# A hybrid decoder step on one core: resident output weights, a ring of six expert rows, diagonals made by VectorE

## The reference, cut to what matters

```python
h = rmsnorm(x, norm1_g); p = h @ w_in                    # 1024 -> 3072 columns
mix = concat([conv_mixer(p), rwkv_mixer(p), sb_attention(p)])
x = x + mix @ w_out                                      # w_out: 1024 x 1024
h2 = rmsnorm(x, norm2_g)
x = x + peer(h2, w_query, sub_keys, u_tab, v_tab)
y = rmsnorm(x, final_g)

def peer_block(xb, w_query, sub_keys, u_tab, v_tab):     # 128 tokens, 8 heads
    s = queries of xb against 2 x 128 keys per head
    s1, i1 = top_k(s[:, :, 0], 16); s2, i2 = top_k(s[:, :, 1], 16)
    top_s, pos = top_k(all 256 sums of s1 and s2, 16)
    e = the 16 experts of pos, out of 16384
    gate = softmax(top_s)
    act = gelu(einsum('thkd,td->thk', u_tab[e], xb))
    return einsum('thk,thkd->td', gate * act, v_tab[e])
```

## Time and profile before

| | us |
|---|---|
| median of 3 runs | 3605.5 |
| lowest and highest run | 3588.62 and 3607.0 |
| the profiled execution's own time | 3601.69 |
| its span, first to last instruction | 3599.9 |
| PE / DVE / ACT / POOL busy in the span | 2793.4 / 2582.6 / 1309.0 / 1381.4 |
| bytes moved by DMA | 1253.82 MB |
| mean granted TensorE clock | 0.866 of full speed |

### The profile page before, as it was taken

One profiled execution on the slowest core, in us unless ns is written; L12 is line 12 of the kernel. 1 busy time (PEld: TensorE's weight loads), 2 busy tenths in 40 slices (PEclk: granted clock), 3 DMA queues, 4 the chain that ended last, 5 costly groups with the idle time before them and its releaser, 6 DMA issues.

```text
span 3599.9 us, 52601 instructions
## 1 busy us (share of the span) xinstructions
PE 2793.4 (78%) x19158; PEld 1375.9 (38%) x19158; DVE 2582.6 (72%) x6413; ACT 1309.0 (36%) x2869; POOL 1381.4 (38%) x1199
## 2 busy tenths in 40 slices
PE   8999877777678767786887678787878777767657
PEld 4555464334244324432443244334433333423211
DVE  2477234878777877788778776887788767677775
ACT  2222122435332543254325532563256323233322
POOL 0000001344453446344544463445444645354443
PEclk9999998888789888988898888888888798788888
DMA  3123354999999999999999999999999999899998
GB/s 96 39 62 92 109 180 178 381 403 384 371 413 400 412 399 408 408 402 416 416 404 398 391 411 399 399 409 414 402 404 405 406 416 410 312 410 410 414 408 342
DMA packets 253683, 1253.82 MB, mean 348 GB/s; under 512 B 63144, under 2 KB 90832, under 8 KB 117744
## 3 DMA queue, kind: packets, MB, share of 16 engines
q0 software_dynamic: 160256, 1132.54, 77.8%
q1 hardware_dynamic: 93168, 117.92, 9.6%
HBM read 1226.84 MB, written 23.53 MB: 347 GB/s over the span
## 4 chain that ended last, share of the span: by engine, by line
PE 27%; DMA 26%; DVE 23%; ACT 5%; issue 4%; POOL 1%; SPq 0%; DVEq 0%; ACTq 0%; POOLq 0%
PE peer_y L2471 13%; DMA uv_first<-in_peer_uv,expert 13%; DMA uv_rows<-in_peer_uv,expert 10%; PE peer_s L2037 5%; DVE uv_first L1775 5%; DVE uv_rows L1775 4%; DMA w_out_rows<-in_w_out 2%; PE scan L2151 2%; PE beside L2077 2%; ACT diag L2012 2%; DVE same L1377 1%; DVE same L1379 1%; DVE pick L1381 1%; DVE weights L1401 1%; ACT L2004 1%
## 5 line engine op out<-in xcount | busy, mean ns | idle before, releaser
L1333 POOL DMA_INDIRECT uv_first<-in_peer_uv,expert x604 | 715.8, 1185 | 1039.9 <-PE peer_y L2471 776.6
L2471 PE MATMUL peer_y<-uv_first,diag 64*64 64x512 f32 x4688 | 742.1, 746 | 390.5 <-ACT diag L2012 376.9
L1775 DVE CUSTOM_DVE_ANT_0 uv_first<-uv_first,p_h 128x1024 f32<-128x1024 f32 x604 | 728.6, 1222 | 204.6 <-DMA uv_first<-in_peer_uv,expert 203.0
L2471 PE MATMUL peer_y<-uv_rows,diag 64*64 64x512 f32 x3504 | 563.2, 751 | 295.8 <-ACT diag L2012 289.1
L1333 POOL DMA_INDIRECT uv_rows<-in_peer_uv,expert x452 | 520.3, 1151 | 676.0 <-PE peer_y L2471 596.9
L1775 DVE CUSTOM_DVE_ANT_0 uv_rows<-uv_rows,p_h 128x1024 f32<-128x1024 f32 x452 | 546.1, 1223 | 139.2 <-DMA uv_rows<-in_peer_uv,expert 138.3
L2004 ACT ACTIVATE gelu<-hidden 128x2 f32<-128x2 f32 x528 | 107.3, 203 | 1209.2 <-DVE hidden L1775 1206.9
L2012 ACT ACTIVATE diag<-p_ident,weights 128x128 f32<-128x128 f32 x1024 | 355.1, 394 | 489.5 <-DVE weights L1401 488.8
L2471 PEld LDWEIGHTS peer_y<-uv_first,diag 64*64 64x64 f32 x4688 | 181.6, 158 | 739.0 <-ACT diag L2012 525.1
L2471 PEld LDWEIGHTS peer_y<-uv_rows,diag 64*64 64x64 f32 x3504 | 136.2, 158 | 561.4 <-ACT diag L2012 406.4
L593 PE MATMUL proj<-mix,w_in_tile 128*128 128x512 f32 x672 | 295.4, 598 | 0.0
(11 more groups left out here) (460 smaller groups left out, 3955.8 us busy)
## 6 DMA issues: line engine op xcount, KB each, us to landing
w_out_rows<-in_w_out SPq DMA_DIRECT2D x50, 512.0 KB, 8.2
w_in_tile<-in_w_in SPq DMA_DIRECT2D x24, 512.0 KB, 3.4
uv_first<-in_peer_uv,expert POOLq DMA_INDIRECT x604
uv_first<-in_w_query SPq DMA_DIRECT2D x8, 1024.0 KB, 7.2
uv_rows<-in_peer_uv,expert POOLq DMA_INDIRECT x452
scan_in<-scratch_scan_in SPq DMA_DIRECT2D x15, 480.0 KB, 8.3
pages_ring<-scratch_k_tiles SPq DMA_DIRECT2D x36, 192.0 KB, 14.2
pages_ring<-out_v_new SPq DMA_DIRECT2D x36, 192.0 KB, 18.5
```

The costliest lines, as they stand in the source:

```text
L1333: pool.indirect_dma_start(out=uv(m, ALL, slice(0, 2 * D)), out_offset=None, in_=io["peer_uv"], in_offset=bass.IndirectOffsetOnAxis(ap=expe ...
L1775: nc.vector.tensor_tensor_reduce(out=uv(m, ALL, slice(0, D)), in0=uv(m, ALL, slice(0, D)), in1=h2[:, b % 2, :], scale=1.0, scalar=0.0, op0 ...
L2471: ins = nc.tensor.matmul(Y[r][rows[j], :], diag[rows[r], m % (2 * GP), rows[r]], uv(m, rows[r], slice(D + j * 512, D + (j + 1) * 512)), st ...
```

## The change

It has these parts.
- **w_out**: all eight slabs have a place of their own (`wo`, [128, 8, 1024]) and are loaded once, by two DMAs of 2 MB. `weights`, `w_out_last` and `w_out_half` are gone.
- **The ring**: six slots in place of seven, one tensor (`uv_ring`).
- **Page slots**: six in place of eight, three for key tiles and three for value tiles. The samples' pages go round by `page_slot`, and beats K_PAGES and V_PAGES are lists.
- **Diagonals**: `weigh` makes them on VectorE, two `tensor_scalar` of 128x64 a group with two per-partition factors (gelu and gate), six slots; ScalarE makes none, and `weights` is gone.
- **Scores**: `choose` reads them in PSUM; `keep` is gone. `score(t + 3)` moves from q = 1 to q = 4 and waits for the last reading of the turn before.
- **final_g**: no longer spread by the load; TensorE spreads it over the rows (`final_gain`, 8 small products) into two PSUM banks once a block, and `normalise` reads it there, at turn 2, q = 6.
- **The samples' state** and other tiles of the samples' attention lie in one tensor with the attention's (`att_units`). The state is loaded before block 6 goes on, and `scan_sample` takes a step every second beat from beat 9.
- In SP's stream the second `scan_load` of a block comes before the store of y.

```diff
-    RING = 7
-    GP = 2
-    PAGES = 8
+    GP, DIAGS = 2, 6
+    PAGES = 6
...
-    K_PAGES, V_PAGES = -4, 5
-    CLOSE, X, SPREAD, H2, TURN, H2T = 24, 33, 34, 35, 35, 37
+    K_PAGES, V_PAGES = (-4, -3, -2, -1, 0, 1, 5, 6), (7, 8, 9, 10, 11, 12, 17, 18)
+    CLOSE, X, SPREAD, H2, TURN, H2T = 24, 33, 34, 35, 35, 38
...
-    S_SCAN, S_TURN = 35, DB - 2
+    W_OUT = DC
+    S_SCAN, S_TURN = 9, DB - 2
...
-    scored = lambda t, q: t + 3 if q == 1 else TURNS
-    kept = lambda t, q: t + 3 if q == 7 else TURNS
+    scored = lambda t, q: t + 3 if q == 4 else TURNS
...
-            if b == S_TURN and n - S_SCAN in range(S_STEPS):
-                scan_sample(n - S_SCAN)
+            if b == S_TURN and n - S_SCAN in range(0, 2 * S_STEPS, 2):
+                scan_sample((n - S_SCAN) // 2)
...
+            for n in range(2):
+                half = slice(n * DC // 2, (n + 1) * DC // 2)
+                sp.dma_start(wo[:, half, :], io["w_out"][:, half, :]).then_inc(wo_in[n], 16)
...
-                if g >= 2:
-                    dve.wait_ge(diag_done, GP * (g - 1))
-                nc.vector.tensor_tensor(wgt[:, g % 2, :], gel[:, g % 2, :], gate[:, t % 4, q * GP:(q + 1) * GP], ALU.mult)\
-                    .then_inc(weights_done, 1)
+                eye, n = (ident4, NS) if last(b) else (ident2, HT)
+                for k in range(GP):
+                    m = g * GP + k
+                    if m >= DIAGS:
+                        dve.wait_ge(uv_free, m - DIAGS + 1)
+                    nc.vector.tensor_scalar(diag[:, m % DIAGS, 0:n], eye[:, 0:n], gel[:, g % 2, k:k + 1], gate[:, t % 4, q * GP + k:q * GP + k + 1],
+                                            ALU.mult, ALU.mult).then_inc(diag_done, 1)
...
-                    act.wait_ge(weights_done, g + 1)
-                    for k in range(GP):
-                        m = g * GP + k
-                        if m >= 2 * GP:
-                            act.wait_ge(uv_free, m - 2 * GP + 1)
-                        nc.scalar.activation(diag[:, m % (2 * GP), 0:n], eye[:, 0:n], ACT.Copy, scale=wgt[:, g % 2, k:k + 1])\
-                            .then_inc(diag_done, 1)
-                    if kept(t, q) < TURNS:
-                        keep(kept(t, q))
...
-                            ins = nc.tensor.matmul(S[mine, 0:HN], h2t[:, c, mine], wk[:, c, head * HN:(head + 1) * HN],
+                            ins = nc.tensor.matmul(scores[mine, :], h2t[:, c, mine], wk[:, c, head * HN:(head + 1) * HN],
...
+            def final_gain(b):
...
+                for c in range(DC):
+                    ins = nc.tensor.matmul(B[c // 4][:, c % 4 * P:(c % 4 + 1) * P], ident[HT:HT + DC, HT + c:HT + c + 1].to_broadcast([DC, P]), gain3,
+                                           start=True, stop=True)
+                ins.then_inc(gain_spread, 1)
```

More of the change, by code:

```diff
@@ L1084, in peer @@
         CB = lambda b: B if b else Y
+        scores = S[:, 0:HN]
         r1_of = lambda n, lo=0: RB[n][:, lo * CH:(lo + PR) * CH].rearrange("p (i c) -> p i c", c=CH)
@@ L1267, in _ @@
                     begin_close(b + 1)
-                    weights(b + 1, 0)
-                    weights(b + 1, 1)
+                if scans(b) and b:
+                    scan_load(b + 2, 1)
+                if b == S_TURN:
+                    scan_load_sample()
                 if b:
@@ L1278, in _ @@
                         scan_load(2, 0)
-                    elif scans(b):
-                        scan_load(b + 2, 1)
-                    if b == S_TURN:
-                        scan_load_sample()
-                    for c in range(2, DC - 1):
-                        weights(b + 1, c)
                 if b == 0:
@@ L1422, in normalise @@
                 dve.wait_ge(R.sem, R.at("recip", b))
-                dve.wait_ge(gain_in, 16)
-                nc.vector.scalar_tensor_tensor(x1[0:n, s, :], x1[0:n, s, :], rstd[0:n, 0:1], gain[0:n, :], ALU.mult, ALU.mult)\
-                    .then_inc(y_ready, 1)
+                dve.wait_ge(gain_spread, b + 1)
+                for k in range(2):
+                    half = slice(k * 512, (k + 1) * 512)
+                    ins = nc.vector.scalar_tensor_tensor(x1[0:n, s, half], x1[0:n, s, half], rstd[0:n, 0:1], B[k][0:n, :], ALU.mult, ALU.mult)
+                ins.then_inc(y_ready, 1)
             def close_x(b):
@@ L1785, in _ @@
                         add_values(b - 1)
-                    if b and h == 1 and q == GROUPS - 2:
+                    if b and (h, q) == NORMED[last(b)]:
                         normalise(b - 1)
@@ L1985, in _ @@
             close_turned(0)
[L1986 to L1987 removed]
+            act.wait_ge(const_in, 16 * 8)
             scan(1, 0, 13)
[L1989 removed]
             scan(1, 0, 14)
@@ L1993, in _ @@
             exps(1)
-            keep(2)
             for t in range(TURNS):
                 b, h = divmod(t, PH)
-                eye = ident4 if last(b) else ident
-                n = rows_of(b)
                 for q in range(GROUPS):
@@ L2475, in _ @@
                         score(scored(t, q))
+                    if b and (h, q) == SPREAD_FINAL[last(b)]:
+                        final_gain(b - 1)
                     if not last(b):
                         beside(b, h * GROUPS + q)
+            pe.wait_ge(y_ready, NBLK - 1)
+            final_gain(NBLK - 1)
 class Resident:
```

187 lines of the change are left out of this document (86 added, 101 removed).

## The result

| | median us | lowest to highest | ratio to before, 95% interval |
|---|---|---|---|
| kernel before, in the same comparison | 3606.25 | 3588.62 to 3607.32 | |
| changed kernel | 3708.86 | 3705.82 to 3712.1 | 1.0296 [1.0263, 1.033] |

The change makes the kernel about 107 us slower by the ratio. The forecast was 3582 us with a range to 3675. The measured time lies outside the range, on the other side.

A forecast was written before the change was run, and what follows sets the result against it. The prediction took the DMA transfers to bound `peer` while enough rows are on their way. Its terms, -66.5 - 12 + 15 + 40 = -23.5 us from 3605.5, gave 3582 us, with a range of 3512 to 3675 us (8 in 10).

The forecast's parts named there:

- What bounds the kernel: Stage `peer`, 700 to 3500 us: transfers fill it at DMA share 1.00 and 402 GB/s; VectorE is the engine nearest to full.
- w_out: Loads of w_out after block 0 go: 27.3 MB fewer at 410 GB/s, -66.5 us.
- The recurrence: Samples' scan in block 6 at half pace lets stalls be made up: -12 us, bounds 0 and -18.3.
- Diagonals on VectorE: Two new instructions a group give VectorE 200 us more work, mostly inside its waits for rows: +15 us (0 to 40).
- The covering wait: The 341 us in which VectorE waits for rows to land, said to hold most of the diagonals' added work.
- The ring of six: One row buffer fewer in `peer`; DMA engines run dry only in the worst groups: +40 us, bounds 0 and 119.
- the forecast's round: One row buffer's cycle from issue to next issue needs 13.9 us, 17.5 with a score; six buffers allow 16.6.
- positive slack: Mean slack of a row buffer's cycle, 16.6 - 13.9 = 2.7 us, positive even with a piece of `choose`.
- The slower rival: In `peer`, VectorE holds landed rows back at pieces of `choose`, slots free late, DMA engines empty: 3665 to 3692 us; chance 0.22.
- the point from which it decides: The slower rival decides from a loss of 78 us on, 0.07 us a pick.
- The lock between issue and diagonals: VectorE's diagonals and GpSimd's issues block each other: VectorE loses 230 us, over half showing, 3600 + 100; chance 0.04.
- What would show each step: Signs: about 1226 MB moved, DMA share near 1.00 (under 0.97: ring fails), diagonal mean near 0.3 us, VectorE busy about 200 us more.

The follow-up runs named there:

- a7_rotate: Changed kernel with seven ring buffers; five slabs of w_out stay and one buffer takes slabs 0, 3 and 6 in turn: 3565.09 us, ratio 0.9898 to the kernel before.
- Run 3: Changed kernel, six buffers, with `choose` cut into eight pieces, one for each group, instead of four: 3649.62 us, ratio 1.0115 to the kernel before.

## Why the prediction was wrong, step by step

**What bounds the kernel.** "The transfers fill the stage" was half right. The DMA engines move a row in about 2.5 us when it is issued in time, and the kernel before needs 2.82 us a pick. 14% of its rows were late already, which a share of 1.00 hides. The eight-buffer run shows that a further 50 us were to be had there.

**w_out: -66.5 forecast, -50 measured.** The bytes were right (27.3 MB). The price was not: about three quarters of it came (-50, 12 us either way, so the miss is just clear of the noise). The forecast counted each byte at 410 GB/s, as if the engines were fed throughout. With 14% of the rows late they were not, which would explain it and is not shown to. The same calculation held for `a7_rotate`, where 12.6 MB cost 30 us (31 forecast), in two comparisons with intervals of 7 and 12 us either way.

**The recurrence: -12 forecast**, not to be told from 0, and 7 us by its places. With six buffers a spread step still takes part in a gap, as block 6 shows.

**Diagonals on VectorE: +15 forecast, -3 ± 6 measured.** The size of the work was right (200 us forecast, 183 in the stretch). Of the cost, even 15 was too much. The covering wait was named and sufficed. ScalarE's 0.69 us also left the round: from dot product to the next issue took 6.4 us instead of 6.8.

**The ring of six: +40 forecast, +168 measured. This is the step that failed**, and its upper bound of 119 failed too. Four parts of it:
- The 10.42 us of flight were taken from the chain of waits. A chain goes through the longest pieces. The mean over all rows is 8.9 us, so queueing was 4.4 us and not 6.
- The bare flight of 5.4 us with its issue is a single row at the end of the stage. With five buffers, where 62% of rows are late, the flight alone is still 6.7 us, with about 1.2 us of issue ahead of it: 7.9. The rest of the forecast's round, 13.9 - 5.4 = 8.5 us for the engines, was right (0.9 + 1.2 + 6.4 = 8.5 with five buffers, 8.6 with six). It was the flight that was too short.
- The mean round was held against the mean allowance, 13.9 against 16.6, and "positive slack" was taken for a fed queue. It is the late rows that cost, and their share doubled from 14 to 32%. They are not only the groups with a score: evening out `choose` alone took away a quarter of them, and in block 6 no score stands between the dot products and the rows' products.
- "Lateness of one round is made up in the next": a row takes 2.5 us at best and the pace is 2.8 to 2.9. There are some 0.3 us a row to make up a gap of several us.

**The slower rival had the mechanism** (VectorE holds landed rows back behind `choose`, slots are freed late, the engines run empty), with the point from which it decides, and its own time of 3665 to 3692 came within 17 us of the 3709. It was given 0.22. Run 3 shows that `choose` is a third of the loss, so it is part of the mechanism and not all of it. That the time came so near is partly luck: 119 us for the ring were 49 too few, and 40 us for VectorE were not there.

**The lock between issue and diagonals** is there, but small. The diagonals of the changed kernel (count, ns least/median/most), and one pair beside an issue:

```profile
L1393 DVE TENSOR_SCALAR diag<-ident_halves,gelu,p_gate x1024: 301/314/551, 618.5 to 3610.1; 128x64 f32<-128x64 f32 x171
```

```profile
720.25 1.35 POOL L1322 DMA_INDIRECT uv_ring<-in_peer_uv,expert  x1 [1.12 <-PE peer_y L2452]
...
721.07 0.58 DVE L1393 TENSOR_SCALAR diag<-ident_halves,gelu,p_gate 128x64 f32<-128x64 f32 x2 [0.27 <-ACT gelu L1987]
```

Of the 1024, the 481 with no indirect DMA's issue beside them took 305 to 316 ns. The 543 beside one took 389 ns on average, and all 131 of 450 ns or more ended 14 to 24 ns after an issue had ended. So a diagonal can be held until the issue is over, by at most 0.24 us, and this is the wide spread that the forecast named as the sign. The price is far under the 230 us given: the second of a pair starts 0.23 us after the first and waits at the same time, so a pair beside an issue takes 0.59 us instead of 0.54, 15 us of VectorE in the whole run. The 128x16 instruction of the earlier trace rows keeps to 233 to 235 ns in all but one case, beside issues or not, and so misled. The three 128x64 ones of the earlier trace rows, which the forecast used for its price, took 473, 306 and 305 ns: the first ended 22 ns behind an issue. GpSimd loses nothing: its issues took 715.8 + 520.3 = 1236 us before and 704.0 + 526.2 = 1230 with the diagonals on VectorE, and the time was the same.

**What would show each step** was mostly right. The diagonal's mean was 352 ns and not 300, in part by that lock. "Under 0.97 means that the ring does not hold" was a poor mark, since 0.97 came with 6% less rate. The rate would have been the mark.

## What to carry over

Where buffers go round between a DMA and several engines, don't hold one good round against the mean allowance. Take the whole distribution from the trace: for each transfer the time between its issue and the landing of the one ahead, and count those issued too late. Here the count was 14% with seven buffers, which was no room to give one away: 1 MB of SBUF for the seventh row was worth 168 us, and w_out at rest only 50. A chain of waits shows long pieces, so means are taken from all pieces. And room that is short can be divided otherwise: five slabs at rest and one that turns saved about half of the bytes and kept the ring of seven.

## What the hardware showed that was not expected

- The rate of the transfers followed the number of rows that could be under way, and above six buffers the DMA share hardly showed it: 340, 379, 402 and 409 GB/s over 700 to 3400 us with five, six, seven and eight buffers, at shares of 0.90, 0.97, 1.00 and 1.00.
- A VectorE tensor_scalar of 128x64 beside GpSimd's issue of an indirect DMA can take 551 ns instead of 311, ending just behind the issue. A pair of them loses 0.05 us on average, not twice that wait.
- A VectorE tensor_scalar of 128x64 with two per-partition factors takes 352 ns on average as the profile counts it (311 with no issue beside it), and two in a row 0.54 us; three in a row had been 0.75. The mean of one is not the cost of one in a row.
- The searches of `choose` read PSUM in the changed kernel and SBUF in the run with diagonals alone. The first rows are PSUM, the second SBUF (count, busy us, mean ns):

```profile
L1345 DVE MAX8 best<-peer_s 128x8 f32<-128x128 f32 x132 | 38.8, 294 | 8.0 <-PE peer_s L2011 7.8
L1346 DVE FIND_INDEX8 where<-best,peer_s 128x8 uint32<-128x128 f32 x132 | 38.3, 290 | 0.0
```

```profile
L1356 DVE MAX8 best<-scores 128x8 f32<-128x128 f32 x132 | 38.3, 290 | 8.4 <-ACT scores L1802 8.3
L1357 DVE FIND_INDEX8 where<-best,scores 128x8 uint32<-128x128 f32 x132 | 37.6, 285 | 0.0
```

4 and 5 ns more for PSUM. The Trainium skill ("VectorE: DVE Perf Modes", section on the TRN2 errata) has 62 cycles more for it. These rows don't bear it out, as the earlier trace rows did not.
